# Twenty modulation products shared with GpSimd, six spreading products moved into the first experts, an unnormalised softmax, and a new order at the end of attention

## The chip, the core and the metric

The program runs on one core of a Trainium2 chip. The time is device time in microseconds, from the first to the last instruction of one execution and what lies around it. Its engines are TensorE (PE: matrix products; PEld is its weight load), VectorE (DVE), ScalarE (ACT), GpSimd (POOL) and SyncE (SP, which here only issues transfers). A 32-bit product appears in the trace as two MATMUL records.

## What is computed

Two layers over 256 tokens of width 1024, all in 32 bits. Layer 0 is a differential attention that also reads 256 context tokens; layer 1 is a pooling mixer. Each is followed by a mixture of 16 experts (two per token) and by layer norms. Scale and shift ("modulation") come from a vector product with a 1024 x 6144 matrix per layer:

```
ml = (jax.nn.silu(c) @ mod_w[i] + mod_b[i])[:, None, :]
sh1, sc1, g1, sh2, sc2, g2 = jnp.split(ml, 6, axis=-1)
hl = xl * (1.0 + sc1) + sh1
...
p = jax.nn.softmax(s, axis=-1)
a = p[0] - lam_full * p[1]
return jnp.einsum('bhqk,bkhe->bqhe', a.astype(v.dtype), v)
...
o = o * lax.rsqrt(jnp.mean(jnp.square(o), axis=-1, keepdims=True) + LN_EPS)
o = o * subln.astype(jnp.float32) * (1.0 - lam_init)
return o.reshape(B, Lq, D_MODEL).astype(q.dtype) @ wo
```

The head norm divides each head by its own root mean square, so a factor that is common to a row of `a` drops out, apart from the epsilon.

## The kernel before

Weights pass through a ring of ten slots of 2 MB. After a prologue (0 to 55 us), an attention stage runs to about 330 us; then layer 0's experts to 774 us, the pooling layer, and layer 1's experts.

**Modulation.** A unit is 1024 x 512 of the matrix. The first four units, which the input needs, go through TensorE. The other 20 (`SUMS`) are summed along k by VectorE: `unit_sum` (lines 1221 to 1235) takes eight instructions, one TENSOR_SCALAR (L1230) and seven SCALAR_TENSOR_TENSOR (L1232), each reading a weight row block and the running sum. What is left, 128 partial sums, is added over partitions by TensorE in five batches of four units (`row_batch`, L538), which land in two row tiles (`rows_sum`, L1243). GpSimd only issues the transfers of these units, into slots 2 and 3 in turn; each waits until the unit two before it is summed (L459).

**The attention loop.** Twenty groups of eight products make k, q and v (L568, L578). VectorE takes k of the latents and q out of PSUM with the rotation (L1272 to L1283), ScalarE the rest. Groups 0 to 9 come first. Then 16 steps follow, one for a pair of head and token tile: in step s TensorE makes group 10+s (while there is one), the turn of the group before, the scores of s (L619), the transposed probabilities of s-2 (L480) and the values of s-3 (L637). VectorE finds the row maximum of s (L1352), and for s-1 takes the reciprocals (L1357), scales the second probabilities (L1359) and combines (L1362), and then sums unit 10+s. The order of every engine is written out by hand. VectorE executes in its own order, so what stands behind a unit's eight instructions waits for them.

**Jobs.** From step 10 to 15, nine jobs spread rows over partitions: `cols_0` and `cols_1` (eight small products each, L663, to columns), `g1`, `gt` and `joint` (a row to all partitions), and `rpart` (router offsets, L699). VectorE copies each out (`job_out`).

**Heads.** `norm_heads(t)` norms tile t's heads; tile 0 is normed in step 15, turned and projected (L655) in step 16, between the last probabilities and values. ScalarE's square root needs a table load (L1035).

**Experts.** Each takes six ring units: 32 records for each half of gate and up (L793), a gather for a later pair (L785), the turned hidden values (L809, bank 7), the down product and, after VectorE's L1554, the scatter (L801). The transfers of the experts' units wait for their ring slots in the order written: slots 2 and 3 for the last sums, slot 4 for v's weights, slots 5 and 6 for the last scores and values, slots 7 to 9 for the heads and the first norm.

## Time and profile before

| | us |
|---|---|
| median of 3 runs | 1278.07 (1276.8 to 1278.51) |
| the profiled execution | 1275.7 |
| its span in the profile | 1273.4 |
| TensorE busy | 1145.6 (90%) |
| VectorE busy | 371.5 (29%) |
| ScalarE busy | 170.8 (13%) |
| GpSimd busy | 23.0 (2%) |

Times in the trace are microseconds from the span's start. "x16" counts instructions. In brackets stands how long the engine sat idle before the row, and what ended it; the profile does not count issuing, waiting and register instructions as busy. The profiled execution's own time is 2.4 us below the median of the runs.

### The profile page before, as it was taken

Reading aid. Unit: us, or ns where it says so; the run is one execution under the profiler, and the core shown is the slowest. Engines: PE = TensorE matmul, PEld = TensorE weight load, DVE = VectorE, ACT = ScalarE, POOL = GpSimd, SP = SyncE. Lnnn points to the kernel's source line nnn. Section 1 sums busy time; section 2 is a strip of 40 time slices with the busy share of each in tenths; the row PEclk is TensorE's granted clock in tenths of the full one; section 3 lists DMA queues with packets and bytes.
Section 4 is the critical chain, followed back from the end, with each engine's and each line's share of the span. In section 5 each row is a group of like instructions: output and inputs, shape, how many; then the busy total and the mean of one; then the engine's idle time right before and its main releaser. Section 6 shows DMA issues by size and latency. Waiting matters only on the chain.

```text
span 1273.4 us, 12436 instructions
## 1 busy us (share of the span) xinstructions
PE 1145.6 (90%) x5317; PEld 506.3 (40%) x5317; DVE 371.5 (29%) x783; ACT 170.8 (13%) x402; POOL 23.0 (2%) x28
## 2 busy tenths in 40 slices
PE   5979989989899999999999987899999999999995
PEld 3434334554543333343333324633433333433331
DVE  1278889864211111111111113411111111111113
...
GB/s 329 290 297 297 328 266 264 321 76 198 317 429 428 427 428 428 428 427 427 427 428 428 427 424 422 289 414 429 427 428 428 428 427 427 427 427 428 428 427 162
DMA packets 54941, 476.18 MB, mean 374 GB/s; under 512 B 5034, under 2 KB 6458, under 8 KB 30308
## 3 DMA queue, kind: packets, MB, share of 16 engines
...
## 4 chain that ended last, share of the span: by engine, by line
PE 72%; DVE 12%; DMA 11%; issue 3%; ACT 2%; SPq 0%; DVEq 0%
PE ps L793 48%; DMA ring<-in_moe_wu 6%; PE ps L785 5%; DMA ring<-in_mod_w 5%; PE ps L801 4%; PE ps L578 3%; PE ps L655 2%; DVE work L1550 2%; DVE ring L1232 2%; DVE extra L1232 2%; DVE work L1554 2%; PE ps L568 1%; DVE modp L1232 1%; PE ps L809 1%; PE ps L480 1%
## 5 line engine op out<-in xcount | busy, mean ns | idle before, releaser
L793 PE MATMUL ps<-ring,tra 128*64 128x512 f32 x2048 | 447.0, 594 | 3.4 <-DMA ring<-in_moe_wu 2.3
L793 PEld LDWEIGHTS ps<-ring,tra 128*64 128x64 f32 x2048 | 145.8, 137 | 299.7 <-issue 292.8
L793 PE MATMUL ps<-ring,work 128*64 128x512 f32 x1024 | 228.7, 598 | 29.2 <-DVE work L1550 29.2
L793 PEld LDWEIGHTS ps<-ring,work 128*64 128x64 f32 x1024 | 83.1, 137 | 154.2 <-issue 117.4
L578 PE MATMUL ps<-ring 128*128 128x512 f32 x256 | 114.1, 601 | 0.0
L1545 DVE TENSOR_TENSOR work<-ps,work 128x512 f32<-128x512 f32 x32 | 22.1, 692 | 283.4 <-ACT work L1116 283.4
L1116 ACT ACTIVATE work<-ps 128x512 f32<-128x512 f32 x32 | 19.1, 597 | 532.5 <-PE ps L793 532.5
L801 PE MATMUL ps<-work,extra 64*128 64x512 f32 x256 | 63.6, 615 | 25.1 <-DVE work L1554 25.1
L1109 ACT ACTIVATE tra<-ps,cols 128x128 f32<-128x128 f32 x128 | 48.2, 456 | 244.0 <-PE ps L785 244.0
L1548 DVE TENSOR_TENSOR work<-work,ps 128x512 f32<-128x512 f32 x32 | 22.0, 686 | 182.5 <-PE ps L793 182.5
L785 PEld LDWEIGHTS ps<-extra,xn 128*128 128x128 f32 x512 | 62.5, 200 | 25.6 <-issue 22.7
L578 PEld LDWEIGHTS ps<-ring 128*128 128x128 f32 x256 | 48.4, 193 | 58.5 <-issue 58.5
L785 PE MATMUL ps<-extra,xn 128*128 128x128 f32 x512 | 68.2, 289 | 2.7 <-DVE extra L1458 2.7
L801 PEld LDWEIGHTS ps<-work,extra 64*128 64x128 f32 x256 | 22.0, 186 | 68.4 <-DVE work L1554 53.3
L1554 DVE TENSOR_TENSOR work<-ps,gt 128x512 f32<-128x512 f32 x16 | 11.1, 691 | 117.0 <-PE ps L793 117.0
L1554 DVE TENSOR_TENSOR work<-ps,rows 128x512 f32<-128x512 f32 x16 | 11.1, 691 | 115.5 <-PE ps L793 115.5
L1232 DVE SCALAR_TENSOR_TENSOR ring<-ring 128x512 f32<-128x512 f32 x56 | 42.1, 752 | 2.0
L1550 DVE COPY work<-ps 128x512 f32<-128x512 f32 x32 | 22.2, 692 | 50.8 <-PE ps L809 50.8
L568 PE MATMUL ps<-ring 128*128 128x512 f32 x64 | 31.3, 641 | 1.8 <-DVE ring L1203 1.8
L1052 ACT ACTIVATE work<-ps,small 128x512 f32<-128x512 f32 x32 | 21.7, 683 | 77.1 <-DVE small L1353 77.1
L1232 DVE SCALAR_TENSOR_TENSOR modp<-ring,modp 128x512 f32<-128x512 f32 x42 | 31.6, 752 | 1.5
L1232 DVE SCALAR_TENSOR_TENSOR extra<-ring,extra 128x512 f32<-128x512 f32 x42 | 31.6, 752 | 1.5
...
## 6 DMA issues: line engine op xcount, KB each, us to landing
...
```

Source lines behind the costliest of these rows:

```text
L568: last = mm(bank(acc_bank(g)), hT[:, k, t * P:t * P + P], w[:, k, :], start=(k == 0), stop=(k == KT - 1))
L578: last = mm(bank(acc_bank(g)), hT[:, k, t * P:t * P + P], w[:, k, :], start=(k == 0), stop=(k == KT - 1))
L655: last = mm(bank(2 * t + h), oT[t][:, k, :], wo[:, k, :], start=(k == 0), stop=(k == KT - 1))
L785: last = mm(bank(bk, 0, P, k * P, k * P + slots), xn[:, c0:c0 + P], sgat[:, t, 0:slots], start=(t == 0), stop=(t == TT - 1), skip_group_ch ...
L793: last = mm(ps[SLOTS * h:SLOTS * h + SLOTS, b, :], lhs(k0 + k), w[:, k, h * NB:(h + 1) * NB], start=(k0 + k == 0), stop=(k0 + k == KT - 1) ...
L801: last = mm(bank(2 * t + h), sw[SLOTS * h:SLOTS * h + SLOTS, t * P:t * P + P], ysb[SLOTS * h:SLOTS * h + SLOTS, :], start=False, stop=True ...
L1109: nc.scalar.activation(xg[i // 2 % 2][:, kk, :], bank(bk, k * P, k * P + P), ACT.Identity, bias=one(bcol[2 * layer], kk, 1), scale=one(aco ...
L1232: ins = v_.scalar_tensor_tensor(out=acc, in0=w[:, k, :], scalar=ck, in1=acc, op0=ALU.mult, op1=ALU.add)
L1545: v_.tensor_tensor(hmid, bank(4), sig, ALU.mult).then_inc(sem("silu_ready"), 1)
L1548: v_.tensor_tensor(hmid, hmid, bank(5), ALU.mult).then_inc(sem("h_ready"), 1)
L1550: v_.tensor_copy(work[:, NB:2 * NB], bank(7)).then_inc(sem("hTt_copied"), 1)
L1554: v_.tensor_tensor(ysb, bank(6), gt[layer], ALU.mult).then_inc(sem("ys_ready"), 1)
```

## The change

1. Of the 20 units GpSimd sums eight (`POOLED`), in halves: four TENSOR_SCALAR of 128x512 in place, a TENSOR_TENSOR of 128x1024 and one or two of 128x512. It loads them itself, half by half, into slot 3. VectorE keeps twelve (`DIRECT`), in groups and steps where it has no rotation, from halves that SP loads into slot 2. The row batches wait for both, and three of the five stand one group later.
2. Of the jobs five stay in the loop; `cols_0` has half of its products. Six (the other half, `cols_1`, two `joint`, `rpart_1`, `gt_1`) are issued in experts 1 to 6 of layer 0, between the down product and the scatter.
3. The softmax's first sum is kept as `lead` and the probabilities are combined without the first normalisation: one large and one small VectorE instruction fewer per step. `norm_heads` multiplies its epsilon by lead squared.
4. The head's weight `subln` becomes the scale of ScalarE's copy, so the norm has one large instruction fewer per tile. Both tiles are normed after the loop: TensorE finishes all probabilities and values before the first projection.

```diff
+POOLED = (1, 3, 5, 8, 11, 13, 16, 18)
+DIRECT = [n for n in range(NSUM) if n not in POOLED]
+
+DIRECT_AT = {2: 0, 3: 2, 6: 4, 7: 6, 8: 7, 9: 9, 12: 10, 13: 12, 16: 14, 17: 15, 18: 17, 19: 19}
+LOADS = [0, ("q", 0), 2, ("v", 0), 4, ("k", 1), 6, 7, 9, ("q", 1), 10, 12, ("v", 1), 14, ("wo", 0), 15, 17, 19, ("wo", 1)]
...
-BATCH_AT = {6: 0, 10: 1, 14: 2, 18: 3, 21: 4}
-
-
-JOBS = ("cols_0", "g1_0", "g1_1", "cols_1", "gt_0", "joint_0", "joint_1", "rpart", "gt_1")
-JOB_AT = {10: (0,), 11: (1,), 12: (2,), 13: (3, 4), 14: (5, 6), 15: (7, 8)}
-JOB_BANK = (6, 6, 6, 7, 6, 6, 7, 6, 7)
+BATCH_AT = {6: 0, 11: 1, 15: 2, 19: 3, 21: 4}
+
+
+JOBS = ("cols_0", "g1_0", "g1_1", "gt_0", "rpart_0", "cols_2", "cols_1", "joint_0", "joint_1", "rpart_1", "gt_1")
+JOB_AT = {10: (0,), 11: (1,), 12: (2,), 13: (3,), 14: (4,)}
+JOB_BANK = (6, 6, 6, 7, 6, 7, 7, 7, 7, 7, 7)
+EARLY_JOBS = 5
...
+            early_used(sp, ("mod", 0))
+            for unit in LOADS:
+                if isinstance(unit, tuple):
+                    load_early(unit)
+                    continue
+                for half in range(2):
+                    i = 2 * DIRECT.index(unit) + half
+                    if i >= 2:
+                        sp.wait_ge(sem("half_summed"), i - 1)
+                    load(sum_stage(2, half), sum_source(unit, half), sem(f"direct_loaded_{half}"))
 
...
+            chain = [0]
+
+            def link(ins):
+
+                chain[0] += 1
+                ins.then_inc(sem("pool_chain"), 1)
+                pool.wait_ge(sem("pool_chain"), chain[0])
+
+            def load_half(i):
+
+                pool.dma_start(sum_stage(3, i % 2), sum_source(POOLED[i // 2], i % 2)).then_inc(sem(f"pooled_loaded_{i % 2}"), 16)
+
+            early_used(pool, ("mod", 2))
+            pool.wait_ge(sem("early_loaded_6"), 16)
+            for i in range(2):
+                load_half(i)
+            pool.wait_ge(sem("cs_ready"), 2)
+            pool.wait_ge(sem("hcols_done"), 4)
+            for i in range(2 * len(POOLED)):
+                n, half = POOLED[i // 2], i % 2
+                pool.wait_ge(sem(f"pooled_loaded_{half}"), 16 * (i // 2 + 1))
+                if half == 0 and n >= SUM_BUFS:
+                    pool.wait_ge(sem("row_done"), (n - SUM_BUFS) // BATCH + 1)
+                w, acc = sum_stage(3, half), sums[n % SUM_BUFS]
+                for k in range(4):
+                    kk = 4 * half + k
+                    last = gp.tensor_scalar(w[:, k, :], w[:, k, :], cs[:, 32 * kk:32 * kk + 1], None, ALU.mult)
+                link(last)
+                link(gp.tensor_tensor(w[:, 0:2, :], w[:, 0:2, :], w[:, 2:4, :], ALU.add))
+                if half == 0:
+                    link(gp.tensor_tensor(acc, w[:, 0, :], w[:, 1, :], ALU.add))
                 else:
-                    pool.wait_ge(sem("summed"), n - 1)
-                pool.dma_start(slot(s).rearrange("p (k n) -> p k n", k=KT), columns(mod_w[layer], m))\
-                    .then_inc(sem(f"sum_loaded_{n % 2}"), 16)
-
-            pool.wait_ge(sem("job_out"), len(JOBS))
+                    link(gp.tensor_tensor(w[:, 0, :], w[:, 0, :], w[:, 1, :], ALU.add))
+                    gp.tensor_tensor(acc, acc, w[:, 0, :], ALU.add).then_inc(sem("pool_summed"), 1)
+                    pool.wait_ge(sem("pool_summed"), i // 2 + 1)
+                if i + 2 < 2 * len(POOLED):
+                    load_half(i + 2)
+
...
-                pe.wait_ge(sem("summed"), BATCH * b + BATCH)
+                pe.wait_ge(sem("half_summed"), 2 * sum(n < BATCH * (b + 1) for n in DIRECT))
+                pe.wait_ge(sem("pool_summed"), sum(n < BATCH * (b + 1) for n in POOLED))
...
-                if 2 <= s < NS + 2:
-                    turn_probs(s - 2)
-                if s >= 3:
-                    values(s - 3)
                 if s == NS:
+                    turn_probs(NS - 2)
+                    values(NS - 3)
+                    turn_probs(NS - 1)
+                    values(NS - 2)
+                    values(NS - 1)
                     turn_heads(0)
                     project(0, 0)
+                elif s < NS:
+                    if s >= 2:
+                        turn_probs(s - 2)
+                    if s >= 3:
+                        values(s - 3)
                 for i in JOB_AT.get(s, ()):
                     job(i)
             project(0, 1)
...
+                if layer == 0 and e - 1 in LATE_JOB:
+                    pe.wait_ge(sem("job_out"), LATE_JOB[e - 1] + 1)
...
+                if layer == 0 and e in LATE_JOB:
+                    job(LATE_JOB[e])
                 pe.wait_ge(sem("ys_ready"), q + 1)
                 scatter(swT[e % 2]).then_inc(sem("scattered"), 1)
...
+                        total = lead[:, t, HPJ * j + h:HPJ * j + h + 1] if n == 0 else sm[:, s % 2, 1:2]
                         nc.scalar.activation(pr[s % 2][:, n, :], bank(score_bank(s) + n), ACT.Exp,
-                                             bias=nb[:, s % 2, n:n + 1], scale=SCALE,
-                                             accum_out=sm[:, s % 2, n:n + 1]).then_inc(sem("exp_done"), 1)
+                                             bias=nb[:, s % 2, n:n + 1], scale=SCALE, accum_out=total).then_inc(sem("exp_done"), 1)
                 if 2 <= s < NS + 2:
...
-                if s == NS - 1:
-                    heads_std(0)
-                if s == NS:
-                    copy_heads(0)
-            heads_std(1)
-            copy_heads(1)
+            for t in range(TT):
+                heads_std(t)
+                copy_heads(t)
...
+                    half = k // 4
+                    if k % 4 == 0:
+                        dve.wait_ge(sem(f"direct_loaded_{half}"), 16 * (u + 1))
+                    w, ck = sum_stage(2, half)[:, k % 4, :], cs[:, 32 * k:32 * k + 1]
                     if k == 0:
-                        ins = v_.tensor_scalar(acc, w[:, 0, :], ck, None, ALU.mult)
+                        ins = v_.tensor_scalar(acc, w, ck, None, ALU.mult)
                     else:
-                        ins = v_.scalar_tensor_tensor(out=acc, in0=w[:, k, :], scalar=ck, in1=acc, op0=ALU.mult,
-                                                      op1=ALU.add)
-                    if k < KT - 1:
+                        ins = v_.scalar_tensor_tensor(out=acc, in0=w, scalar=ck, in1=acc, op0=ALU.mult, op1=ALU.add)
+                    if k % 4 == 3:
+                        ins.then_inc(sem("half_summed"), 1)
+                        dve.wait_ge(sem("half_summed"), 2 * u + half + 1)
...
-                v_.tensor_scalar(ss[:, t, :], ss[:, t, :], 1.0 / P, EPS, ALU.mult, ALU.add).then_inc(sem("ss_ready"), 1)
+                link(v_.scalar_tensor_tensor(out=lead[:, t, :], in0=lead[:, t, :], scalar=EPS, in1=lead[:, t, :], op0=ALU.mult,
+                                             op1=ALU.mult))
+                v_.scalar_tensor_tensor(out=ss[:, t, :], in0=ss[:, t, :], scalar=1.0 / P, in1=lead[:, t, :], op0=ALU.mult,
+                                        op1=ALU.add).then_inc(sem("ss_ready"), 1)
                 dve.wait_ge(sem("ostd_ready"), t + 1)
                 link(v_.reciprocal(ors[:, t, :], ors[:, t, :]))
                 o3 = osb[:, t, :].rearrange("p (h n) -> p h n", h=HEADS)
-                link(v_.tensor_tensor(o3, o3, ors[:, t, :].unsqueeze(2).to_broadcast([P, HEADS, P]), ALU.mult))
-                v_.tensor_tensor(o3, o3, subln.unsqueeze(1).to_broadcast([P, HEADS, P]), ALU.mult)\
+                v_.tensor_tensor(o3, o3, ors[:, t, :].unsqueeze(2).to_broadcast([P, HEADS, P]), ALU.mult)\
                     .then_inc(sem("o_normed"), 1)
 
...
+                    if w == "0":
+                        norm_columns(0, 0, SC2, SH2, 1).then_inc(sem("cols_ready"), 1)
+                        dve.wait_ge(sem("cols_ready"), 1)
+                        dve.wait_ge(sem("router_loaded"), 48)
+                        scaled_router(0)
+                    elif w == "1":
+                        link(norm_columns(1, 1, SC1, SH1, 0))
+                        v_.tensor_scalar(flat, bcol[1][:, 0].rearrange("p q h -> p h q"), cst[:, C_FLAT:C_FLAT + 1], None,
+                                         ALU.mult)
+                        norm_columns(2, 1, SC2, SH2, 1).then_inc(sem("cols_ready"), 1)
...
-                    link(v_.reciprocal(rs[:, b, :], sm[:, b, :]))
-                    link(v_.tensor_tensor(rl[:, b:b + 1], rs[:, b, 1:2], lam[:, 5:6], ALU.mult))
-                    link(v_.tensor_scalar(pr[b][:, 1, :], pr[b][:, 1, :], rl[:, b:b + 1], None, ALU.mult))
+                    j, t, h = STEPS[s - 1]
+                    link(v_.reciprocal(rs[:, b, 1:2], sm[:, b, 1:2]))
+                    link(v_.scalar_tensor_tensor(out=rl[:, b:b + 1], in0=rs[:, b, 1:2], scalar=lead[:, t, HPJ * j + h:HPJ * j + h + 1],
+                                                 in1=lam[:, 5:6], op0=ALU.mult, op1=ALU.mult))
                     if s >= 3:
                         dve.wait_ge(sem("aT_done"), s - 2)
-                    v_.scalar_tensor_tensor(out=att[b], in0=pr[b][:, 0, :], scalar=rs[:, b, 0:1], in1=pr[b][:, 1, :],
+                    v_.scalar_tensor_tensor(out=att[b], in0=pr[b][:, 1, :], scalar=rl[:, b:b + 1], in1=pr[b][:, 0, :],
                                             op0=ALU.mult, op1=ALU.add).then_inc(sem("att_ready"), 1)
-                if 10 + s < NSUM:
-                    unit_sum(10 + s)
...
-                if s == NS - 1:
-                    norm_heads(0)
-            norm_heads(1)
+            for t in range(TT):
+                norm_heads(t)
...
+                if layer == 0 and e in LATE_JOB:
+                    job_out(LATE_JOB[e])
```

GpSimd, its whole program up to the second half of the first unit: before, then in the change (`in_mod_w` is the modulation matrix, `modp` a tile for sums). Both pieces begin at its branch into the block.

```order
L450 UNCONDITIONAL_BRANCH
L459 DMA ring<-in_mod_w 128x8x512 x20
L467 ISA
L467 TENSOR_TENSOR ring<-ring,modp 128x512 x4
L162 UNCONDITIONAL_BRANCH
```

```order
L481 UNCONDITIONAL_BRANCH
L494 DMA ring<-in_mod_w 128x4x512 x2
L510 ISA
L510 TENSOR_SCALAR ring<-ring 128x512 x4
L512 TENSOR_TENSOR ring<-ring 128x1024
L514 TENSOR_TENSOR modp<-ring 128x512
L494 DMA ring<-in_mod_w 128x4x512
L510 TENSOR_SCALAR ring<-ring 128x512 x4
L512 TENSOR_TENSOR ring<-ring 128x1024
L516 TENSOR_TENSOR ring<-ring 128x512
L517 TENSOR_TENSOR modp<-modp,ring 128x512
```

Where GpSimd's program held only transfers, 13 instructions a unit now stand between them.

VectorE in step 1 of the loop, from the rotation of group 11 on: before, then in the change (`ps` is PSUM, `work` the probabilities, `tra` the combined ones, `extra` a tile for sums).

```order
L1272 TENSOR_TENSOR ring<-ps,ring 128x512
L1280 TENSOR_TENSOR ring<-ps,ring 128x8x16 x4
L1283 TENSOR_TENSOR ring<-ring 128x512
L1352 TENSOR_REDUCE small<-ps 128x2
L1353 TENSOR_SCALAR small<-small 128x2
L1357 RECIPROCAL small<-small 128x2
L1358 TENSOR_TENSOR small<-small 128x1
L1359 TENSOR_SCALAR work<-work,small 128x512
L1362 SCALAR_TENSOR_TENSOR tra<-work,small 128x512
L1230 TENSOR_SCALAR extra<-ring 128x512
L1232 SCALAR_TENSOR_TENSOR extra<-ring,extra 128x512 x7
```

```order
L1349 TENSOR_TENSOR ring<-ps,ring 128x512
L1357 TENSOR_TENSOR ring<-ps,ring 128x8x16 x4
L1360 TENSOR_TENSOR ring<-ring 128x512
L1440 TENSOR_REDUCE small<-ps 128x2
L1441 TENSOR_SCALAR small<-small 128x2
L1446 RECIPROCAL small<-small 128x1
L1447 SCALAR_TENSOR_TENSOR small<-small 128x1
L1451 SCALAR_TENSOR_TENSOR tra<-work,small 128x512
```

In this step the unit's eight instructions and the scaling of the probabilities are gone; the next unit follows only in step 2.

TensorE at the end of attention: before, then in the change (`cst` is the identity, `tra` the probabilities, L655 and L716 the projections).

```order
L480 MATMUL ps<-cst,tra 128x128 x4
L637 MATMUL ps<-ring,tra 128x128 x4
L480 MATMUL ps<-cst,ring 128x128 x8
L655 MATMUL ps<-ring 128x512 x8
L480 MATMUL ps<-cst,tra 128x128 x4
L637 MATMUL ps<-ring,tra 128x128 x8
L655 MATMUL ps<-ring 128x512 x8
L480 MATMUL ps<-cst,ring 128x128 x8
L655 MATMUL ps<-ring,tra 128x512 x16
```

```order
L698 MATMUL ps<-ring,tra 128x128 x4
L540 MATMUL ps<-cst,tra 128x128 x4
L698 MATMUL ps<-ring,tra 128x128 x8
L540 MATMUL ps<-cst,ring 128x128 x8
L716 MATMUL ps<-ring 128x512 x16
L540 MATMUL ps<-cst,ring 128x128 x8
L716 MATMUL ps<-ring,tra 128x512 x16
```

The turn of the last probabilities and eight value products moved from between the first two projections to ahead of the first turn of heads.

## Rows read from the trace of the kernel before

**Rows 1.** Busy us (PE, PEld, DVE, ACT, POOL) by stretch; clock, DMA, GB/s.

```profile
75.00:100.00 25.00, 17.86 (x46) 8.28 (x44) 16.95 (x27) 2.08 (x4) 2.65 (x3) 0.88 0.99 365
58.72:235.87 177.15, 158.43 (x488) 73.09 (x486) 151.45 (x256) 32.24 (x85) 15.92 (x18) 0.95 0.76 274
235.87:266.72 30.85, 28.20 (x133) 17.36 (x132) 28.28 (x68) 14.15 (x48) 0.00 (x0) 0.83 0.65 264
343.00:756.00 413.00, 386.46 (x1892) 154.34 (x1888) 58.09 (x128) 32.12 (x74) 0.00 (x0) 1.00 1.01 428
```

**Rows 2.** Waits of TensorE in 55:245: total us, times, longest.

```profile
PE ps L480 <- DVE ring L1283: 10.2, 2, 7.1
...
PE ps L538 <- DVE rows L1243: 5.4, 1, 5.4
...
PE ps L619 <- ACT work L1052: 3.1, 2, 1.9
```

**Rows 3.** Timeline of TensorE, attention loop: start us, us, what [idle before <-releaser].

```profile
75.07 7.03 PE L578 MATMUL ps<-ring 128*128 128x512 f32 x16
...
97.45 8.79 PE L578 MATMUL ps<-ring 128*128 128x512 f32 x16
...
146.75 1.13 PE L619 MATMUL ps<-ring 64*128 64x512 f32 x4 [1.86 <-ACT work L1052]
...
182.74 2.08 PE L619 MATMUL ps<-ring 64*128 64x512 f32 x4
```

**Rows 4.** VectorE: idle ahead of line 1230; then groups, 56:276: busy, mean ns.

```profile
  DMA ring<-in_mod_w: 14.4, 7
...
L1232 DVE SCALAR_TENSOR_TENSOR ring<-ring 128x512 f32<-128x512 f32 x56 | 42.1, 752 | 2.0
...
L1230 DVE TENSOR_SCALAR extra<-ring 128x512 f32<-128x512 f32 x6 | 2.9, 484 | 7.9 <-DMA ring<-in_mod_w 7.9
```

**Rows 5.** Groups of GpSimd, whole span: count, busy us, mean ns, idle before.

```profile
L459 POOL DMA_DIRECT2D ring<-in_mod_w x20 | 17.9, 893 | 206.5 <-DVE ring L1232 66.5 <-DVE modp L1232 61.6 <-DMA ring<-in_mod_w 41.2
L467 POOL TENSOR_TENSOR ring<-ring,modp 128x512 f32<-128x512 f32 x4 | 4.9, 1262 | 545.0 <-DMA ring<-in_pool_w 545.0
```

**Rows 6.** Timeline of VectorE: the last of the first column outputs.

```profile
53.22 0.17 DVE L1213 TENSOR_SCALAR cols<-ps 128x8 f32<-128x8 f32 x1 [4.59 <-PE ps L526]
```

**Rows 7.** Timeline of TensorE, end of the attention loop.

```profile
239.44 2.84 PE L663 MATMUL ps<-cst,rows 128*128 128x28 f32 x16
...
243.47 0.62 PE L538 MATMUL ps<-modp,cst 128*32 128x512 f32 x2 [1.19 <-DVE extra L1232]
...
249.59 1.13 PE L619 MATMUL ps<-ring 64*128 64x512 f32 x4
...
253.00 1.13 PE L619 MATMUL ps<-ring 64*128 64x512 f32 x4
```

**Rows 8.** Chain that ended last, around the head norms: start us, us, what.

```profile
271.74 1.28 ACT L1035
...
274.77 1.24 DVE ring L1297
...
287.43 0.44 PE ps L480 x4
...
287.87 0.91 PE ps L637 x8
...
290.59 6.87 PE ps L655 x16
```

**Rows 9.** Timeline of TensorE: expert 1's scatter, and the stage's last transfer wait.

```profile
388.90 1.99 PE L801 MATMUL ps<-work,extra 64*128 64x512 f32 x8 [0.78 <-DVE work L1554]
...
756.92 3.65 PE L793 MATMUL ps<-ring,tra 128*64 128x512 f32 x16 [1.04 <-DMA ring<-in_moe_wu]
```

**Rows 10.** Timeline of GpSimd and VectorE around one issue.

```profile
110.88 0.88 POOL L459 DMA_DIRECT2D ring<-in_mod_w  x1 [7.30 <-DVE ring L1232]
111.33 0.66 DVE L1230 TENSOR_SCALAR ring<-ring 128x512 f32<-128x512 f32 x1 [0.74 <-DMA ring<-in_mod_w]
```

131 lines of the change are left out of this document (70 added, 61 removed).

## The prediction

> **What bounds the kernel now.** I read the table of stretches first, then TensorE's waits and its timeline through the attention loop, then the chain. The experts are out of reach of most of the change: from 343 to 756 TensorE is busy 386.5 of 413 us at full clock, while transfers run at 428 GB/s [rows 1]. Both are full, and both start when attention ends: TensorE with the first gather, the transfers with the last ring slots that attention frees. So what attention saves arrives at the end one for one, as long as the last slots come free earlier with it. The attention loop is what can give: between 58.72 and 235.87 VectorE is busy 151.5 of 177 us and TensorE 158.4, the transfers move 274 GB/s [rows 1]. TensorE is near its own bound here; what it loses are a few waits. Three lie behind VectorE's rotation or unit sums: 10.2 us before turns (two waits), 5.4 before a row batch, and 3.1 before scores, whose softmax starts late for the same reason [rows 2]. After the long ones TensorE's clock is granted at its lower level (1.2 GHz instead of 2.4) for a while: a group takes 8.79 us where another takes 7.03, scores 2.08 where they take 1.13 [rows 3]. Together 10.2 + 5.4 + 3.1 + 1.8 + 0.9 = 21.4 us. After step 10 the loop has no more groups, and VectorE is busy 28.3 of 30.9 us [rows 1].
>
> **A: the loop to step 10.** A unit costs VectorE 0.48 + 7 x 0.75 = 5.8 us [rows 4]. Eight of twenty leave, seven of them inside the stretch (40 us), and the scaling of the probabilities, an instruction of the same form as L1230 (0.48 us, about ten of them); no unit is left in a step with a rotation, and unit 0 comes after the second rotation. That takes away what held TensorE in all three places, so the ceiling is 21.4 us. What is late next is a transfer or a GpSimd sum.
>
> GpSimd: its only arithmetic here is TENSOR_TENSOR 128x512, 1.26 us; a transfer issue costs 0.89 [rows 5]. TENSOR_SCALAR on GpSimd is not in the trace. Its bounds are VectorE's 0.48 [rows 4] and GpSimd's own two-input 1.26 [rows 5]; I take the middle, 0.87, since it is the same engine with one input fewer. 128x1024 is taken as twice 1.26. A unit is then 8 x 0.87 + 2 x 2.52 + 3 x 1.26 + 2 x 0.89 + 0.4 for waits = 18 us (14.9 to 21.1). It starts at about 54, after the last column output [rows 6]. Two units are done at 90, eight at 198. TensorE reaches the first row batch at 97.45 + 8.79 + 0.5 = 106.7 before [rows 3], less the turn waits of 10.2 and the slow clock of 1.8 ahead of it: 94.7. So GpSimd is in time by 5 us, and at its slow bound (96) 1 us late; the last batch, at about 224, is met at either bound (198 to 223).
>
> The Trainium skill, "GPSIMD Engine Reference", section "Performance versus the Vector engine", gives 0.77 us as the best case for 512 elements in a one-input loop. By it a unit would be 17.2 us instead of 18 and the sum would not move. No run so far shows it.
>
> Transfers: 274 GB/s over 177 us is 48.5 MB [rows 1]. The same bytes in some 160 us need 303 GB/s; the loop's best stretch moved 365 at a DMA share of 0.99 [rows 1]. It fits, but not always in time: VectorE sat idle 14.4 us in seven waits for units [rows 4], some 2 us each, and SP now issues in one order units and weights (wk, wq, wv, wo), so that a weight whose slot is free can stand behind a half unit that is not. Units 6, 7 and 9, and again 15, 17 and 19, follow each other in the groups and steps without rotation, with VectorE itself at nearly TensorE's pace. I put back three such waits, 6 us; the ends are 0 and the full 21.4. A = -15.4, and step 10 starts at 220.5.
>
> **B: steps 10 to 15.** They take 30.85 us [rows 1]. A step with little in it takes 253.00 - 249.59 = 3.4 [rows 7]. Five of them are 17.1. Added: half of the column products, 2.84 / 2 = 1.4 [rows 7], the row batch, 1.1, and 1.4 for a slow clock (the granted clock is 0.83 on average in this stretch [rows 1]). That makes 21, with VectorE's column arithmetic and four copies gone from under it. B = -9.9. Ends: 17.1 + 1.4 (-12.4), and -5 if each step keeps a wait on ScalarE.
>
> **C: the heads.** Before, the table load at 271.74 opens the norm of tile 0; the norm's second pass, 1.24, stands in the chain; and between the projections stand 290.59 - 287.43 = 3.2 us of probabilities and values [rows 8]. Both go (-4.4). Now the last probabilities come first: combining (about 1.1), turn 0.44, copy 0.6, values 0.91 [rows 8], and the square about 0.5, before the table load: +3.1 over before, some of it beside VectorE's copies. Tile 1's norm lies under two projections of 6.9 us. C = -1.3 (ends -3 and +2).
>
> **D: the six late jobs.** Between the down product and the scatter TensorE waits 0.78 us for VectorE [rows 9]; a job there is free up to that. The half of the columns costs 1.42 - 0.78 = 0.6, `cols_1` 2.84 - 0.78 = 2.1 [rows 7]; `gt_1`, two products like the scores' 1.13 [rows 3], 0.35; a `joint` and `rpart_1` nothing. VectorE's copies follow its scatter factor and have the 14 us of the next gate and up products; TensorE's new wait before the hidden turn stands behind those. D = +3.0 (0 to +5; the stage already ends on a transfer wait of 1.04 us [rows 9], so a part may fall into it).
>
> **Sum.** -15.4 - 9.9 - 1.3 + 3.0 = -23.6: the profiled execution would go from 1275.7 to 1252.1. It stands 2.4 below the median, so the predicted median is 1254.5.
>
> **Rivals.**
> *1. VectorE is held by GpSimd's reads (slower).* Place: the seven two-input instructions of each unit, 84 in all. If each waits until a GpSimd instruction has ended, and GpSimd has always one ready, the price is the mean of its 13 per unit, 15.8 / 13 = 1.2 us. VectorE's load to step 10 is 151.5 - 7 x 5.8 - 10 x 0.48 = 106 us without it, and 207 with it: step 10 at 266, A = +30, the sum +21.8 and the time 1299.9. It decides from about 0.9 us each: A must reach +8.2, step 10 at 244.1, which leaves (185.4 - 106) / 84 = 0.94. Below 0.66 it hides. For it: the one VectorE instruction of this form that ran beside a GpSimd issue took 0.66 instead of 0.48 us, and it is one that reads SBUF alone [rows 4, 10]. Against it: the sums' two-input instructions average 752 ns although twenty issues fell among them [rows 4, 5], so an issue does not hold them; whether a GpSimd instruction that reads does, no row tells.
> The Trainium skill, "SBUF — State Buffer", section "Who interferes with whom", says that a VectorE instruction with two SBUF inputs and a GpSimd instruction that reads SBUF exclude each other for the whole instruction; by that rule this rival is the forecast. The trace neither shows nor contradicts it.
> *2. Supply: transfers or GpSimd late.* If the staging halves hide less than the former pairs of slots, or GpSimd needs 21 us a unit and the batches wait, more than half of A is lost: A = -7, and the median is 1262.9. For it: a loop stretch already runs at 0.99 of the DMA engines [rows 1]. Against it: the mean of the loop is 0.76.
> *3. The experts do not start earlier at the end.* If the transfer stream sets the end of layer 0 and its start does not move, nothing arrives: 1278. For it: the 1.04 us wait for a transfer in the last expert [rows 9]. Against it: the slots that start the stream are freed by the scores, values, heads and first norm, which all move.
>
> **From cases to numbers.** Forecast 0.57, its own range 1246 to 1262; supply 0.20; no gain 0.07; held by GpSimd 0.16. About 0.2% (2.6 us) is what a measurement of this kernel can tell from no change. Faster: 0.57 + 0.20 = 0.77; same 0.07; slower 0.16. Low end: A in full (-21.4), B -12.4, C -3, D +1 give -36 and 1242; I take 1241. The high end reaches half-way into rival 1, where each instruction waits about 1.0 us: 1284.
>
> **What would show it.** Right: TensorE's waits before turns, row batches and scores (L480, L538, L619 before) gone, groups at 7.0 us from 60 to 210, step 10 near 220, the heads' table load near 250, the first gather near 303, jobs visible as 0.5 to 2 us in experts 1, 2 and 6. GpSimd units 18 us apart, busy from 54 to 198. Wrong in A: the sums' seven instructions over 0.75 us each (rival 1), or VectorE waiting for `in_mod_w` by more than 14 us, or TensorE idle before a row batch (rival 2). Wrong in D: experts 1 to 6 longer than the others by more than 5 us together. The prediction as a whole fails if step 10 starts after 235.

## The result, and the profile after

The changed kernel takes 1292.5 us (median of 4 runs, 1288.4 to 1293.8) against 1278.3 (4 runs): ratio 1.012, 95% interval 1.009 to 1.015. It is slower; 1254.5 was forecast, and the range (1241 to 1284) does not hold it.

The spans cut at four points, in us (step 10's scores, step 15's scores, first gather, end), with the forecast's own points:

| profiled run | to step 10 | 10 to 15 | to first gather | to the end | span |
|---|---|---|---|---|---|
| before | 235.9 | 30.9 | 63.3 | 943.4 | 1273.4 |
| forecast | 220.5 | 21.0 | 62.0 | 946.4 | 1249.8 |
| after | 248.2 | 31.9 | 66.0 | 944.4 | 1290.5 |

So +12.4, +1.1, +2.7 and +1.0, where -15.4, -9.9, -1.3 and +3.0 stood. The stretches of after, busy us of PE, PEld, DVE, ACT, POOL, then clock, DMA share and GB/s, as in [rows 1]:

```profile
58.72:248.23 189.51, 162.96 (x494) 74.83 (x492) 168.13 (x179) 32.07 (x85) 181.65 (x112) 0.92 0.70 244
248.23:280.15 31.92, 22.84 (x121) 13.77 (x120) 29.28 (x53) 12.55 (x43) 6.00 (x4) 0.79 0.86 329
```

VectorE runs 179 instructions where it ran 256 and is busy longer: 168.1 us against 151.5. The groups in 56:300 say why (busy, mean ns, idle before):

```profile
L510 POOL TENSOR_SCALAR ring<-ring 128x512 f32<-128x512 f32 x63 | 105.6, 1687 | 0.7
L1308 DVE SCALAR_TENSOR_TENSOR ring<-ring 128x512 f32<-128x512 f32 x42 | 55.9, 1331 | 1.5
L512 POOL TENSOR_TENSOR ring<-ring 128x1024 f32<-128x1024 f32 x16 | 39.3, 2456 | 1.3
L1308 DVE SCALAR_TENSOR_TENSOR modp<-ring,modp 128x512 f32<-128x512 f32 x21 | 28.1, 1339 | 0.7
L1308 DVE SCALAR_TENSOR_TENSOR extra<-ring,extra 128x512 f32<-128x512 f32 x21 | 26.0, 1239 | 1.2 <-DMA ring<-in_mod_w 0.5
...
L1360 DVE TENSOR_TENSOR ring<-ring 128x512 f32<-128x512 f32 x8 | 10.4, 1299 | 0.3
L1306 DVE TENSOR_SCALAR ring<-ring 128x512 f32<-128x512 f32 x6 | 8.9, 1485 | 1.4 <-DMA ring<-in_mod_w 1.4
```

A sum's instruction (L1308) takes 1.31 us on average where [rows 4] had 0.75; the one-input start of a sum (L1306) 1.49 instead of 0.48; the add that ends a rotation (L1360) 1.30 instead of 0.69. VectorE's rotation instructions that read PSUM stayed at 0.69. GpSimd's TENSOR_SCALAR takes 1.69, where the forecast took 0.87. TensorE waits behind the rotations, and for transposed probabilities that ScalarE copies (total, times, longest, in 55:345), as in [rows 2]:

```profile
PE ps L540 <- DVE ring L1360: 24.0, 3, 10.1
PE ps L540 <- ACT tra L1135: 10.6, 5, 7.6
```

and the timeline, against [rows 3, 7, 8], has slow products after each of them, at step 10 one wait more for probabilities that VectorE made late (256.92), and a late and slow first projection (296.57):

```profile
153.19 1.11 PE L540 MATMUL ps<-cst,ring 128*128 128x128 f32 x4 [10.11 <-DVE ring L1360]
...
156.22 2.08 PE L680 MATMUL ps<-ring 64*128 64x512 f32 x4
...
248.23 1.13 PE L680 MATMUL ps<-ring 64*128 64x512 f32 x4
...
256.92 1.09 PE L540 MATMUL ps<-cst,tra 128*128 128x128 f32 x4 [7.56 <-ACT tra L1135]
...
280.15 1.13 PE L680 MATMUL ps<-ring 64*128 64x512 f32 x4
...
290.68 1.28 ACT L1110 ACT_TABLE_LOAD   x1
293.73 1.97 PE L540 MATMUL ps<-cst,ring 128*128 128x128 f32 x8 [3.63 <-DVE ring L1377]
...
296.57 16.80 PE L716 MATMUL ps<-ring 128*128 128x512 f32 x32 [0.87 <-ACT ring L1117]
```

In the same trace the profile puts no wait of TensorE down to a sum of GpSimd: GpSimd's last unit ends at 254.5, and TensorE comes to the batch that needs it at 261.4, where it waits another 0.5 us for VectorE.

### The profile page after: what moved, and what is told of

It is laid out like the page before. It is cut to its first block, busy times and chain, and to the rows that moved or that the text cites. A ratio compares the mean times of both kernels' runs of the same rounds, so it can differ in the third digit from the quotient of the medians.

```text
span 1290.5 us, 12519 instructions
## 1 busy us (share of the span) xinstructions
PE 1150.5 (89%) x5317; PEld 508.8 (39%) x5317; DVE 390.5 (30%) x705; ACT 171.1 (13%) x402; POOL 200.0 (15%) x128
## 4 chain that ended last, share of the span: by engine, by line
PE 73%; DVE 16%; DMA 6%; issue 3%; ACT 2%; ACTq 1%; DVEq 0%
PE ps L864 50%; PE ps L856 5%; PE ps L872 5%; DVE ring L1308 3%; DMA ring<-in_moe_wd 3%; PE ps L716 2%; DVE modp L1308 2%; PE ps L629 2%; DMA ring<-in_mod_w 2%; DVE extra L1308 2%; DVE work L1638 2%; DVE work L1642 1%; PE ps L880 1%; PE ps L639 1%; PE ps L540 1%
## 5 line engine op out<-in xcount | busy, mean ns | idle before, releaser
L639 PE MATMUL ps<-ring 128*128 128x512 f32 x256 | 114.7, 603 | 0.0
L510 POOL TENSOR_SCALAR ring<-ring 128x512 f32<-128x512 f32 x64 | 107.3, 1686 | 10.9 <-PE ps L586 10.1
L527 POOL TENSOR_TENSOR ring<-ring,modp 128x512 f32<-128x512 f32 x4 | 5.0, 1270 | 531.7 <-DMA ring<-in_pool_w 531.7
L1308 DVE SCALAR_TENSOR_TENSOR ring<-ring 128x512 f32<-128x512 f32 x42 | 55.9, 1331 | 1.5
L512 POOL TENSOR_TENSOR ring<-ring 128x1024 f32<-128x1024 f32 x16 | 39.3, 2456 | 1.3
L540 PE MATMUL ps<-cst,ring 128*128 128x128 f32 x80 | 14.5, 326 | 27.6 <-DVE ring L1360 24.0
```

What stands on the lines that cost most here:

```text
L510: last = gp.tensor_scalar(w[:, k, :], w[:, k, :], cs[:, 32 * kk:32 * kk + 1], None, ALU.mult)
L512: link(gp.tensor_tensor(w[:, 0:2, :], w[:, 0:2, :], w[:, 2:4, :], ALU.add))
L540: last = nc.tensor.transpose(bank(b, 0, P, k * P, k * P + P), src[:, k * P:k * P + P], ident)
L639: last = mm(bank(acc_bank(g)), hT[:, k, t * P:t * P + P], w[:, k, :], start=(k == 0), stop=(k == KT - 1))
L1308: ins = v_.scalar_tensor_tensor(out=acc, in0=w, scalar=ck, in1=acc, op0=ALU.mult, op1=ALU.add)
```

## The experiments

The kernel before was run again beside each group of experiments and took 1275.6 to 1280.6 us (medians); each ratio is to that, and small differences are safer read from the ratios than from the times.

**Parts 2 to 4 alone (e1_parts_2_to_4).** The changed kernel with part 1 taken back:

```
-DIRECT_AT = {2: 0, 3: 2, 6: 4, ...}
+DIRECT_AT = {n: n for n in range(NSUM)}
-BATCH_AT = {6: 0, 11: 1, 15: 2, 19: 3, 21: 4}
+BATCH_AT = {6: 0, 10: 1, 14: 2, 18: 3, 21: 4}
 (GpSimd issues the 20 units' transfers again, VectorE sums them)
```

> Parts 2 to 4 of the change without part 1: VectorE sums all twenty units again from the two old slots, GpSimd only issues transfers, the batches stand where they stood before. Theory P (shared reads: the whole loss lies in part 1): the sums' instructions are back at 0.75 us, step 10 starts within 3 us of 235.9, then B saves 6 to 10 us, C 0 to 3 and D costs 3 to 5: the time is 3 to 8 us below before, about 1272. Rival T (parts 2 to 4 themselves cost, through the late jobs or the head order): the time is above before, 1280 to 1285.

Measured: 1271.3, ratio 0.997 (0.995 to 0.998). All of VectorE's two-input sums take 0.752 us again. What loses is part 1; but these three parts bring 4 us, not the 8.2 of B + C + D. The profiled execution was the slowest of the thirteen (1280.8), so its stretches are weak evidence: step 10 starts at 241.9 (expected within 3 of 235.9), steps 10 to 15 take 26.1, and from there to the first gather 65.0.

**GpSimd without its sums (e2_pool_loads_only).** It issues its transfers and does one MEMSET of the sum per unit; the products of those eight units are left out.

```
-    last = gp.tensor_scalar(w[:, k, :], w[:, k, :], cs[...], None, ALU.mult)
-    link(gp.tensor_tensor(...)) ...
+    link(gp.memset(acc, 0.0))
```

> The change with GpSimd's eight sums left out: it loads its halves as before, and writes zeros to its sum tile (one write-only instruction a unit); eight modulation units are therefore missing from the result. Theory P: VectorE's sums run at 0.75 us, the rotations no longer wait, step 10 starts near 215 to 220 and the time is about 1250 to 1256. Rival S (supply: the halves and the single SP order of units and weights hold the loop): VectorE or TensorE wait for transfers by more than 15 us in the loop, step 10 stays later than 230 and the time above 1265.

Measured: 1254.9, ratio 0.983 (0.981 to 0.986), the forecast's own figure. Its VectorE groups, then TensorE at steps 10 and 15:

```profile
L1302 DVE SCALAR_TENSOR_TENSOR ring<-ring 128x512 f32<-128x512 f32 x42 | 31.6, 752 | 9.0 <-DMA ring<-in_mod_w 7.5
```

```profile
218.36 1.13 PE L674 MATMUL ps<-ring 64*128 64x512 f32 x4
...
242.36 1.13 PE L674 MATMUL ps<-ring 64*128 64x512 f32 x4
```

Step 10 starts at 218.4 (forecast 220.5). So all of the miss in A comes with GpSimd's arithmetic. The supply was judged less well than the sum suggests: VectorE waits 25.2 us in all for units here (14.4 before), far over the 6 us that A put back and over the 14 us that were named as a sign of failure, but TensorE reaches step 10 in time all the same.

**A small kernel that times the two engines (m1_ports).** Not the model; 128x512 instructions alone and side by side.

> Not the model: single instructions of VectorE and GpSimd, 128x512 in 32 bits, alone and side by side, each waiting for the one before it. Theory P: GpSimd's one-input product is 1.55 us alone; VectorE's two-input sum from SBUF takes 0.75 us alone, and beside GpSimd's one-input product about 0.75 + 0.8 = 1.5 on average; beside GpSimd's memset (writes only) 0.75; a sum whose second input and output are PSUM 0.75 beside the product; a one-input product SBUF to SBUF of VectorE, 0.48 alone, is held as well; one from SBUF to PSUM is not. Rival W (it is not the read but any GpSimd instruction, or its writes): the memset holds VectorE as well. Rival I (only the issue of instructions, semaphores and waits are slow beside a busy GpSimd): the PSUM forms are held as much as the SBUF forms.

Lines 70, 133 and 137 ran alone, the pairs 77/145, 81/149, 85/153 and 97/165 side by side:

```profile
L70 DVE SCALAR_TENSOR_TENSOR acc<-src,col,acc 128x512 f32<-128x512 f32 x8 | 6.0, 752 | 0.3
L133 POOL TENSOR_SCALAR gout<-gin,col 128x512 f32<-128x512 f32 x8 | 12.5, 1565 | 6.0 <-DVE fd L62 5.4
L137 POOL TENSOR_TENSOR gout<-gin 128x512 f32<-128x512 f32 x8 | 10.1, 1262 | 0.7
L77 DVE SCALAR_TENSOR_TENSOR acc<-src,col,acc 128x512 f32<-128x512 f32 x16 | 14.5, 906 | 12.2 <-POOL fp L124 11.6
L145 POOL TENSOR_SCALAR gout<-gin,col 128x512 f32<-128x512 f32 x14 | 24.0, 1712 | 1.4 <-POOL fp L124 0.2
L81 DVE SCALAR_TENSOR_TENSOR acc<-src,col,acc 128x512 f32<-128x512 f32 x16 | 12.0, 752 | 10.9 <-POOL fp L124 10.4
L85 DVE SCALAR_TENSOR_TENSOR ps<-src,col,ps 128x512 f32<-128x512 f32 x16 | 12.1, 756 | 8.2 <-POOL fp L124 7.6
L97 DVE SCALAR_TENSOR_TENSOR acc<-src,col,acc 128x512 f32<-128x512 f32 x16 | 24.3, 1521 | 3.0 <-POOL fp L124 2.4
L165 POOL TENSOR_TENSOR gout<-gin 128x512 f32<-128x512 f32 x14 | 22.4, 1600 | 1.2
```

GpSimd's TENSOR_SCALAR alone takes 1.565 us, outside the forecast's bounds (0.48 to 1.26). Beside its TENSOR_TENSOR VectorE's two-input instruction takes 1.52, beside TENSOR_SCALAR 0.91, beside a MEMSET 0.75, and with the sum in PSUM 0.76. The 1.5 expected beside TENSOR_SCALAR was missed. VectorE's one-input instruction was not timed beside a MEMSET.

**Busy, but not reading (e3_pool_memsets).** Every arithmetic instruction of GpSimd becomes one or two MEMSETs of about its length, each waiting for the one before; the eight units are left out.

```
-    last = gp.tensor_scalar(w[:, k, :], w[:, k, :], cs[...], None, ALU.mult)
+    link(gp.memset(flat_w[:, 0:1740], 0.0))
-link(gp.tensor_tensor(w[:, 0:2, :], w[:, 0:2, :], w[:, 2:4, :], ALU.add))
+link(gp.memset(flat_w[:, 0:1400], 0.0))   # twice
```

> The changed kernel with every arithmetic instruction of GpSimd replaced by MEMSETs of about its length (1740 elements for a TENSOR_SCALAR, 1400 for a TENSOR_TENSOR): GpSimd is as busy, writes as much or more, and reads nothing; its eight units are left out of the result. Theory P (VectorE's sums wait for GpSimd's reads): the sums take 0.75 us again, step 10 starts at 205 to 212, and the time is 1253 to 1262, near the 1254.9 of the run without GpSimd's sums; a GpSimd unit takes 20 us, and the last row batches may wait a few us for it. Rival O (any work of GpSimd holds VectorE, or the transfers, or the batches wait for GpSimd anyhow): the sums stay at 1.2 to 1.3 us and the time at 1285 to 1293.

Measured: 1278.4, ratio 1.002 (1.000 to 1.003). Groups and TensorE's timeline:

```profile
L510 POOL MEMSET ring<- 128x1740 f32 x64 | 100.7, 1574 | 14.1 <-PE ps L588 11.3
L1310 DVE SCALAR_TENSOR_TENSOR ring<-ring 128x512 f32<-128x512 f32 x42 | 31.6, 752 | 8.4 <-DMA ring<-in_mod_w 7.1
L1308 DVE TENSOR_SCALAR ring<-ring 128x512 f32<-128x512 f32 x6 | 5.1, 847 | 7.6 <-DMA ring<-in_mod_w 7.6
```

```profile
223.66 1.13 PE L682 MATMUL ps<-ring 64*128 64x512 f32 x4
249.63 1.07 PE L601 MATMUL ps<-modp,cst 128*32 128x512 f32 x2 [17.14 <-POOL extra L519]
```

The two-input sums are back at 0.752, the rotations' adds at 0.69 and step 10 at 223.7: it is the reads that hold these. The one-input starts are not free: they take 0.86 us on average beside MEMSETs (12 of them, 10.3 us; 0.48 without), so what holds them is not the reads alone. The time was missed by both theories: the last row batch waits 17.1 us for GpSimd. That is a second cause, GpSimd's length.

How the 37.6 us between 1254.9 and 1292.5 divide is known only roughly. By this run the length costs 1278.4 - 1254.9 = 23.5 us and the reads 14 more, but the MEMSETs are too long: a unit follows the other every 24.5 us, where GpSimd's own instructions unhindered, with the issues and gaps of the first unit of e5_psum_sums, make 23.7 (an estimate: 8 x 1.565 + 2 x 2.34 + 3 x 1.262 + 2 x 0.81 + 1.1). Over eight units that is some 6 us, so nearer 17 for the length and 20 for the reads. And the two do not simply add: in the changed kernel the holds make everything late enough that no wait for GpSimd is left. Short GpSimd instructions that read as much as these were not run.

**A second small kernel (m2_ports).** Is it GpSimd's gapless rows of four that hold VectorE longer in the kernel (1.31) than in the first small one (0.91)?

> Not the model: a small kernel that times VectorE and GpSimd instructions of 128x512 alone and side by side; its outputs are of no use. Question: in the changed kernel VectorE's two-input sums take 1.24 to 1.33 us, in the first small kernel only 0.91 beside GpSimd's TENSOR_SCALAR (but 1.52 beside its TENSOR_TENSOR). There every GpSimd instruction waited for the one before; in the kernel four follow without a wait. Theory L (it is this): beside TENSOR_SCALAR issued four in a row VectorE's instruction takes 1.5 us, in place or not. Rival: it stays at 0.9, and what holds in the kernel is GpSimd's TENSOR_TENSOR alone. Memsets two in a row: 0.75 by the theory that only reads hold, more if the missing gap alone does it. VectorE with sum in PSUM: 0.75 beside either. VectorE's one-input TENSOR_SCALAR beside GpSimd's TENSOR_TENSOR: 0.48 if only two-input instructions are held, 0.8 or more if all are that read and write SBUF. GpSimd's product as a TENSOR_TENSOR with the column broadcast, alone: 1.26 like the other (then it is cheaper than TENSOR_SCALAR's 1.565), or 1.57 if the multiplier's operand costs.

Line 131 ran alone, 78 beside TENSOR_SCALARs four in a row and in place, the pair 86/153 side by side, and 90 beside TENSOR_TENSOR:

```profile
L153 POOL TENSOR_TENSOR gout<-gin,col 128x512 f32<-128x512 f32 x12 | 16.6, 1380 | 1.0
L86 DVE SCALAR_TENSOR_TENSOR acc<-src,col,acc 128x512 f32<-128x512 f32 x12 | 16.3, 1354 | 6.3 <-POOL fp L117 5.9
L90 DVE TENSOR_SCALAR acc<-src,col 128x512 f32<-128x512 f32 x16 | 14.8, 926 | 1.5 <-POOL fp L117 1.0
L78 DVE SCALAR_TENSOR_TENSOR acc<-src,col,acc 128x512 f32<-128x512 f32 x12 | 10.9, 906 | 10.1 <-POOL fp L117 9.8
L131 POOL TENSOR_TENSOR gout<-gin,col 128x512 f32<-128x512 f32 x6 | 6.2, 1038 | 0.5 <-DVE fd L62 0.2
```

No: four in a row, in place, gives 0.906 again; that theory fell. New: VectorE's one-input instruction inside SBUF is held too (0.93), and GpSimd's product as TENSOR_TENSOR with the column broadcast takes 1.04 alone, two thirds of TENSOR_SCALAR.

**A third (m3_ports).** Mixture, shared scalar or transfers?

> Not the model: a third small kernel, VectorE's unit of sums (one TENSOR_SCALAR, seven two-input instructions) beside GpSimd, in four stretches: (1) beside GpSimd's TENSOR_SCALAR four in a row with the same scalar tile, (2) with a scalar tile of its own, (3) beside GpSimd's whole pattern of the changed kernel: four TENSOR_SCALAR, one TENSOR_TENSOR of 1024, one of 512, (4) the same while transfers write another part of SBUF. Open: in the changed kernel VectorE's sums take 1.24 to 1.33 us and GpSimd's TENSOR_SCALAR 1.56 back to back, in the small kernel 0.91 and 1.73. Theory M (the mixture does it): 0.9 in stretches 1 and 2, 1.2 to 1.35 in 3 and 4. Rival X (the transfers do it): 1.2 or more in stretch 4 only. Rival S (the shared scalar): 0.75 in stretch 2.

Stretch 2 (L85), 3 (L91) and 4 (L97), then the first two units of stretch 3 one by one:

```profile
L97 DVE SCALAR_TENSOR_TENSOR acc<-src,col,acc 128x512 f32<-128x512 f32 x21 | 24.5, 1168 | 0.7
L91 DVE SCALAR_TENSOR_TENSOR acc<-src,col,acc 128x512 f32<-128x512 f32 x21 | 24.5, 1168 | 0.7
L85 DVE SCALAR_TENSOR_TENSOR acc<-src,col,acc 128x512 f32<-128x512 f32 x14 | 13.0, 927 | 0.5
67.48 6.71 DVE L91 SCALAR_TENSOR_TENSOR acc<-src,col,acc 128x512 f32<-128x512 f32 x7
74.83 9.23 DVE L91 SCALAR_TENSOR_TENSOR acc<-src,col,acc 128x512 f32<-128x512 f32 x7
```

It is the mixture: beside TENSOR_SCALAR alone 0.93, beside the kernel's pattern 1.17, with or without transfers. The mean of 1.17 holds one unit of three that met only TENSOR_SCALARs (6.71 us for seven, 0.96 each); the other two take 9.23, 1.32 each, and three units of the changed kernel take 9.25 to 9.26. So the pattern alone gives the kernel's 1.31.

**The sum in PSUM (e5_psum_sums).** The complete changed kernel; VectorE's six units before step 0 accumulate in a bank that is free until then.

```
+    part = bank(5) if u < 6 else acc
-    ins = v_.scalar_tensor_tensor(out=acc, in0=w, scalar=ck, in1=acc, ...)
+    ins = v_.scalar_tensor_tensor(out=acc if k == KT - 1 else part, in0=w, scalar=ck, in1=part, ...)
```

> The changed kernel, complete, with one thing changed: VectorE's first six units (0, 2, 4, 6, 7, 9), summed before step 0, accumulate in a free PSUM bank, only their last instruction writes SBUF, so that each instruction has one SBUF input. Theory P: their 42 two-input instructions fall from 1.3 to 0.75 us (22 us of VectorE), GpSimd's unit beside them from 25.5 to about 21, step 0 starts 12 to 20 us earlier, part of it is given back where the row batches wait for GpSimd's late units; the time is 1270 to 1282. Rival (the hold is not about the sum's SBUF operand): durations and time stay, 1287 to 1294.

Measured: 1282.7, ratio 1.005 (1.003 to 1.007), 8 to 10 us under the changed kernel and just above the expected range; step 10 at 233.7. Early and late units of one kernel:

```profile
L1309 DVE SCALAR_TENSOR_TENSOR ps<-ring,ps 128x512 f32<-128x512 f32 x36 | 27.2, 756 | 10.9 <-DMA ring<-in_mod_w 9.7
L1309 DVE SCALAR_TENSOR_TENSOR ring<-ring 128x512 f32<-128x512 f32 x21 | 25.0, 1190 | 2.2 <-DMA ring<-in_mod_w 1.5
```

The holds on the early units are gone, but step 0 starts at 130.0, only 4.9 us earlier than in the changed kernel (12 to 20 expected): VectorE now waits 18.3 us for the transfers of these units.

**A faster GpSimd (e8_broadcast_products).** The complete changed kernel, GpSimd's 64 products as TENSOR_TENSOR.

```
-    last = gp.tensor_scalar(w[:, k, :], w[:, k, :], cs[:, 32 * kk:32 * kk + 1], None, ALU.mult)
+    last = gp.tensor_tensor(w[:, k, :], w[:, k, :], cs[:, 32 * kk:32 * kk + 1].to_broadcast([P, NB]), ALU.mult)
```

> The changed kernel, complete, with GpSimd's 64 TENSOR_SCALAR (1.56 us alone) made TENSOR_TENSOR with the column broadcast (1.04 alone, 1.38 beside VectorE, which it holds to 1.41 each). Theory (GpSimd's length sets the row batches and the hold lasts as long as the instruction): a GpSimd unit takes 22 to 23 us instead of 25.5, VectorE's sums stay at 1.3 to 1.4, the last unit is done some 20 us earlier, and the time falls to 1280 to 1290. Rival (a tighter exclusion costs VectorE more than GpSimd's earlier end gives): 1293 to 1300.

Measured: 1316.2, ratio 1.033 (1.030 to 1.035), beyond both expectations. Groups, and TensorE's longest wait:

```profile
L510 POOL TENSOR_TENSOR ring<-ring 128x512 f32<-128x512 f32 x64 | 67.0, 1081 | 57.1 <-PE ps L599 47.3 <-PE ps L586 9.5
L1308 DVE SCALAR_TENSOR_TENSOR ring<-ring 128x512 f32<-128x512 f32 x42 | 62.8, 1495 | 1.5
```

```profile
PE ps L540 <- DVE ring L1360: 44.9, 2, 25.4
```

GpSimd is near its speed alone (1.08) and VectorE pays (1.50 on the ring group): the stronger exclusion is worse than the shorter instruction is good, and TensorE waits 44.9 us behind rotations. GpSimd then waits 47.3 us itself, behind three row batches.

**The old order of heads (e4_heads_as_before).** Parts 2 to 4, without the new order of part 4 (tile 0's norm again at step 15, ahead of the last values).

```
+                if s == NS - 1:
+                    norm_heads(0)
+            norm_heads(1)
-            for t in range(TT):
-                norm_heads(t)
```

> Parts 2 to 4 of the change without part 1 (the run of 1271.3), and with the order of values, heads and first projections put back as before (tile 0's norm at step 15 ahead of the last values). From step 15's start to the first gather it was 63.3 us before and 64.9 with the new order. Theory C+ (the new order costs): the stretch falls to 62 to 63.5, and the time to 1269 to 1270 (0.995 of before). Rival C- (the forecast's term, -1.3 for the new order): the stretch grows to about 66 and the time is 1272.5.

Measured: 1267.8, ratio 0.994 (0.992 to 0.996). Step 15, the table load and the first gather:

```profile
256.75 0.70 PE L638 MATMUL ps<-ring 64*128 64x512 f32 x2
...
261.76 1.28 ACT L1062 ACT_TABLE_LOAD   x1
...
316.82 6.46 PE L808 MATMUL ps<-extra,xn 128*128 128x128 f32 x32 [1.37 <-DVE extra L1500]
```

From step 15 to the gather 60.1 us, where it was 65.0 in the run of parts 2 to 4 and 63.3 before (over all runs 65.0 to 66.1 with the new order, 60.1 to 63.4 with the old one). So the new order costs about 5 us between the two profiled executions; the medians lie 3.5 us apart, and their intervals overlap. Against before, the stretch is 3 us shorter without the new order; which of the other parts saves that was not separated.

**The late jobs back in the loop (e7_jobs_in_loop).** On top of the last; six jobs stand in steps 13 to 15, closer together than they stood before.

```
-JOB_AT = {10: (0,), 11: (1,), 12: (2,), 13: (3,), 14: (4,)}
+JOB_AT = {10: (0,), 11: (1,), 12: (2,), 13: (3, 4, 5), 14: (6, 7, 8), 15: (9, 10)}
```

> Parts 2 to 4 with the order of heads as before (the run of 1267.8), and now the six late jobs back in steps 13 to 15 of the loop. There the trace had: steps 10 to 15 24.1 us (30.85 before the change), from the first gather to the end 945.8 (943.4 before). Theory D (moving the jobs is worth more than it costs): steps 10 to 15 and the stretch to the first gather grow by 4 to 7 us together, the end is won back by 2.4, and the time is 1270 to 1273. Rival (the jobs lay hidden behind VectorE and ScalarE in the loop, and the late ones only cost): the time falls to 1264 to 1266.

Measured: 1273.2, ratio 0.999 (0.997 to 1.000), so against this placing moving them is worth 5.4 us. Steps 10 to 15 take 34.8 us instead of 24.1 (30.9 before, with the jobs spread wider), and the end 942.9 instead of 945.8.

**Two complete versions.** From these: GpSimd sums few units, early, beside VectorE sums in PSUM; heads in the old order; late jobs kept.

```
+POOLED = (1, 3, 5, 7)          # e6;  (1, 3, 5, 7, 10) in e9
+EARLY_DIRECT = 6               # e6;  7 in e9: units that accumulate in bank 5
+last = gp.tensor_tensor(w[:, k, :], w[:, k, :], cs[...].to_broadcast([P, NB]), ALU.mult)   # GpSimd's products, both
+STAGE = [...]                  # once GpSimd is done, VectorE's units alternate between both slots
```

> A complete version built from the findings: GpSimd sums four units only (1, 3, 5, 7), its products as TENSOR_TENSOR with the column broadcast (1.04 us alone); VectorE's six units before step 0 accumulate in PSUM, so neither holds the other; the other ten units are VectorE's alone, from both slots, at the steps after GpSimd has ended; order of values and heads as before the change; late jobs kept. Theory P with the forecast's arithmetic: GpSimd's unit takes about 20 us, the last is done at about 135, the sums take 0.75 us throughout, step 10 starts at 218 to 225, steps 10 to 15 take 24 to 28, from there to the first gather 60, the rest 945: 1250 to 1260 (0.98 to 0.99 of before). Rival (supply: ten units of VectorE at the loop's end wait for transfers that stand behind weights in SP's order): step 10 after 232 and 1266 or more, no gain on the version with parts 2 to 4 and the old order of heads (1267.8).

Measured: 1268.5, ratio 0.994 (0.992 to 0.997). Step 10 at 220.2 as expected; but steps 10 to 15 take 37.4 us, two units of sums and the gate rows' copies behind them. The first half was right, the place of the last units wrong. So a fifth unit went to GpSimd:

> A complete version after the last one (1268.5), which came to step 10 at 220.2 as expected but took 37.4 us for steps 10 to 15, because two units of VectorE and the last row batch stood at steps 10, 11 and 13 and the gate rows' copies behind them. Now GpSimd sums a fifth unit (10) between 134 and 155, beside at most one rotation and a unit of VectorE in PSUM; VectorE has one unit left at step 10, behind the column copy; the last row batch is at step 12, the jobs at steps 10 to 14. Theory P with the trace's arithmetic: sums 0.75 us but for the few beside GpSimd's fifth unit, step 10 at 219 to 224, steps 10 to 15 24 to 28, to the first gather 60 to 63, the rest 944: 1251 to 1260. Rival (the units were not the cause, or GpSimd's fifth unit holds VectorE at a place where TensorE waits): steps 10 to 15 stay over 33, or step 10 is after 228, and the time is 1264 to 1270.

Measured: 1263.5, ratio 0.988 (0.986 to 0.990), above the expected range, but the fastest complete version, 1.2% under before. VectorE's sums and rotation adds in it, and the stretches to step 10 and to step 15:

```profile
L1312 DVE SCALAR_TENSOR_TENSOR ps<-ring,ps 128x512 f32<-128x512 f32 x42 | 31.7, 756 | 1.5
...
L1312 DVE SCALAR_TENSOR_TENSOR ring<-ring 128x512 f32<-128x512 f32 x28 | 21.1, 752 | 1.0
L1365 DVE TENSOR_TENSOR ring<-ring 128x512 f32<-128x512 f32 x8 | 12.8, 1597 | 0.3
```

```profile
58.72:222.04 163.32, 158.32 (x496) 72.96 (x497) 127.54 (x201) 32.55 (x86) 87.18 (x69) 0.98 0.82 293
222.04:251.89 29.85, 20.91 (x121) 12.64 (x120) 28.45 (x57) 12.52 (x43) 0.00 (x0) 0.89 0.63 248
```

To step 10 TensorE is busy 158.3 of 163.3 us. Steps 10 to 15 still take 29.9 us instead of the expected 24 to 28, with one unit of VectorE in them. GpSimd's reads are not free here either: the rotations' adds, which have two SBUF operands, take 1.60 us instead of 0.69, and VectorE waits 18.0 us for the transfers of its PSUM units.

## Why the prediction was wrong

**A, the step that failed.** It gave GpSimd's arithmetic a length of 0.87 us and no effect on VectorE. Both were wrong, and together they cost 37.6 us (1254.9 to 1292.5), of which an estimated 17 to 23 belong to the length and 14 to 20 to the holds. The length: TENSOR_SCALAR takes 1.565 us alone, more than the two-input instruction, which the forecast had set as the upper bound ("the same engine with one input fewer"); a unit then takes 23.7 us, not 18 (25.4 in the changed kernel, where VectorE slows GpSimd too), and with the somewhat longer MEMSETs the last row batch comes 17.1 us late (1278.4). The last unit was to be done at 198 and is done at 254.5. The reads: a share of 0.16 stood on them as rival 1, whose mechanism is what happened; the MEMSET and PSUM runs show it in the kernel. Its size and its path were off too. The hold is 0.56 us per two-input sum on average, 84 x 0.56 = 47 us, not 1.2 each; but it also takes the 12 starts (17.2 - 12 x 0.48 = 11 us) and the rotations' adds (8 x 0.61 = 5 us), which the rival left out. And below 0.66 it was to hide, which 0.56 does not. Nor do all 84 sums lie before step 10, as the rival's load had it; 75 do. VectorE's load there comes out as 106 - 9 (what now falls behind step 10) + 44 (75 sums) + 12 (starts) + 5 (adds) + 10 (smaller instructions of the softmax, as L1447, 128x1: 0.73 us for 0.22) = 168 us, as measured (168.1), in a stretch of 189.5: the rival's sum let VectorE work without a gap, while the holds fall on the rotations, for which TensorE waits (24.0 us) and whose delay reaches VectorE's next work again.

The Trainium skill, "SBUF — State Buffer", section "Who interferes with whom", has a VectorE instruction with two SBUF inputs contend with a GpSimd instruction that reads SBUF, and not with one that only writes. For two-input instructions every run here agrees. An exclusion for the whole instruction, as the prediction read it, fits TENSOR_TENSOR (1.52) and not TENSOR_SCALAR (0.91). The same section says that VectorE's `tensor_scalar` can take the shared ports too; the starts of the sums agree (0.48 to 1.49 us, and 0.86 beside MEMSETs, which only write), and the prediction had read past that sentence. The forecast set that rule's case at 0.16 because no row showed it; a row that does not show a case is no evidence against it.

**Rival 2 (supply)** was half right: GpSimd was late, as the run with MEMSETs shows. VectorE waited only 3 us in all for units (14.4 before), but because it was slow itself: in the run without GpSimd's sums it waited 25.2 us, at no visible cost for TensorE.

**B** was -9.9; where GpSimd does not hold VectorE it is -6.8 (24.0 us without its sums, 24.1 with the old heads; 26.1 for parts 2 to 4). Over the 17.1 of bare steps stand 6.9 us, not 3.9. The slow clock is not among them (the granted clock is 1.00 in that stretch of the run without sums); in its place come waits, 3.5 us for ScalarE's copies and 1.6 for a sum of VectorE ahead of the batch, which were only in the upper bound. In the changed kernel itself it is +1.1, for the wait of 7.6 at step 10 behind VectorE's sums is A's damage in B's stretch.

**C** was -1.3 and is +2.7. The new order puts ScalarE's table load 10.5 us behind step 15's scores (5.0 before): three turns, copies, values and squares one after the other, +5.5 where +3.1 was counted. Then TensorE waits 3.6 us before the heads are turned (3.1 before), and the first projection of 16.8 us (15.7 in two pieces before, 14.1 in the run with the old order) starts at the lower clock (0.83 granted on average), which was not in the sum.

**D** was +3.0. From expert 0's scatter to expert 7's it takes 195.8 us where it took 191.6, so +4.2 at first; at the end +1.0 is left. `cols_1` costs 2.0 in expert 2, as counted, and 1.9 more in expert 3: behind its small products the scatter takes 3.15 us instead of 1.99, at a granted clock of 0.61. The other jobs are nearly free. TensorE's waits for transfers fall from 2.3 to 1.2 us, which gives part of it back; the rest was not traced. What the jobs free in the loop stands in B; against the placing of e7_jobs_in_loop it is 10.7 us of steps 10 to 15.

The sum without GpSimd's arithmetic came out at 1254.9 for a forecast of 1254.5, but by errors that cancel: B and C came out worse by 7.1, A and D better by 4.1, and 2.0 us lie between span and median there, not 4.7.
